# A new order of row gathers, two blocks fewer visited early, and other places for the steps woven between them

## The reference

```python
s_top, i_top = lax.top_k(scores, PEER_TOPK)          # twice 128 keys, 16 of each
best, pos = lax.top_k(cand, PEER_TOPK)               # 16 of the 256 pairs
u = u_tab[ib]
act = gelu(einsum("td,thkd->thk", tb, u))            # a dot product for each row
out = einsum("thk,thkd->td", gb * act, v_tab[ib])
x = x + out
```

```python
u = h @ w_up                                         # 1024 -> 5632, 22 pairs of 128 columns
u = up[:, :-2]*conv_w[0] + up[:, 1:-1]*conv_w[1] + up[:, 2:]*conv_w[2] + conv_b
return (silu(a) * v) @ w_down                        # 2816 -> 1024
```

## Time and profile before

| what | us |
|---|---|
| median of 3 runs | 1692.13 (1692.06 to 1692.37) |
| profiled execution | 1692.13 |
| its span | 1690.2 |
| TensorE matmuls busy | 1488.3 (88%) |
| VectorE busy | 1043.8 (62%) |
| GpSimd busy | 745.1 (44%) |
| ScalarE busy | 529.0 (31%) |
| mean granted TensorE clock | 0.942 |

### The profile page before, as it was taken

One profiled execution on the slowest core, in us unless ns is written; L12 is line 12 of the kernel. 1 busy time (PEld: TensorE's weight loads), 2 busy tenths in 40 slices (PEclk: granted clock), 3 DMA queues, 4 the chain that ended last, 5 costly groups with the idle time before them and its releaser, 6 DMA issues.

```text
span 1690.2 us, 22536 instructions
## 1 busy us (share of the span) xinstructions
PE 1488.3 (88%) x8510; PEld 1046.8 (62%) x8510; DVE 1043.8 (62%) x2210; ACT 529.0 (31%) x839; POOL 745.1 (44%) x676
## 2 busy tenths in 40 slices
PE   8999999846566777885999999998699999999999
PEld 7997675734222333432855555544399986799987
DVE  5865633797597866787677775431244157568864
ACT  6653331211121121113322210002133164466652
POOL 0025220476667777775346665655000013027650
PEclk9999999978787789997999999999799999999999
DMA  7447860698999999999999999999668756635551
GB/s 277 150 150 314 316 230 25 249 394 295 401 406 371 378 381 390 405 406 355 335 386 383 378 374 401 340 342 337 230 211 285 265 215 257 216 134 191 172 195 42
DMA packets 161308, 489.51 MB, mean 290 GB/s; under 512 B 10160, under 2 KB 14000, under 8 KB 158000
## 3 DMA queue, kind: packets, MB, share of 16 engines
q0 software_dynamic: 73728, 268.47, 41.4%
q1 hardware_dynamic: 87472, 219.60, 35.7%
HBM read 486.98 MB, written 1.05 MB: 289 GB/s over the span
## 4 chain that ended last, share of the span: by engine, by line
PE 60%; POOL 10%; DMA 9%; DVE 8%; issue 5%; ACT 2%; another core or an unknown queue 1%; DVEq 0%; ACTq 0%; POOLq 0%
PE ps L761 59%; POOL arena L3096 8%; DMA arena<-in_peer_v,cl 5%; DVE arena L2028 2%; POOL wring L3096 2%; PE ps L765 2%; DMA wring<-in_ups 1%; DMA wring<-in_peer_v,cl 1%; DVE arena L1642 1%; DVE arena L1648 1%; ACT arena L2439 1%; DMA arena<-in_peer_u,arena 1%; DMA wring<-in_attn_w_qkv 0%; DVE arena L1645 0%
## 5 line engine op out<-in xcount | busy, mean ns | idle before, releaser
L761 PE MATMUL ps<-arena,wring 128*32 128x512 f32 (+6 forms) x3048 | 713.0, 461 | 101.7 <-DMA arena<-in_peer_v,cl 85.8
L761 PEld LDWEIGHTS ps<-arena,wring 128*128 128x128 f32 (+1 forms) x3048 | 402.7, 172 | 390.8 <-DMA arena<-in_peer_v,cl 154.0
L3096 POOL DMA_INDIRECT arena<-in_peer_u,arena x214 | 243.2, 1136 | 257.2 <-PE ps L761 117.4
L2028 DVE CUSTOM_DVE_ANT_0 arena<-arena 128x1024 f32<-128x1024 f32 x214 | 255.9, 1225 | 118.8 <-DMA arena<-in_peer_u,arena 101.1
L3096 POOL DMA_INDIRECT arena<-in_peer_v,cl x214 | 229.8, 1074 | 96.7 <-issue 62.0
L2439 ACT ACT_TABLE_LOAD x68 | 87.2, 1283 | 354.6 <-DVE arena L2028 162.7
L1648 DVE SCALAR_TENSOR_TENSOR cvs<-ps,vec,cvs 128x255 f32<-128x255 f32 (+3 forms) x240 | 105.3, 439 | 59.5 <-ACT cvs L2439 47.3
L761 PE MATMUL ps<-hhl,wh 128*128 128x256 f32 (+1 forms) x528 | 126.2, 322 | 0.6 <-POOL hhl L3106 0.4
L761 PEld LDWEIGHTS ps<-arena 128*128 128x128 f32 (+1 forms) x708 | 88.4, 198 | 50.5 <-issue 29.5
L761 PE MATMUL ps<-arena 128*128 128x128 f32 (+4 forms) x708 | 100.1, 295 | 22.1 <-ACT arena L2442 8.0
L1642 DVE TENSOR_TENSOR wl<-wring,wh 128x2048 fp32r<-128x2048 f32 (+1 forms) x42 | 92.1, 2193 | 37.7 <-ACT wh L2442 36.8
(11 more groups left out here) (279 smaller groups left out, 2219.4 us busy)
## 6 DMA issues: line engine op xcount, KB each, us to landing
wring<-in_ups SPq DMA_DIRECT2D x38, 2048.0 KB
wring<-in_ada SPq DMA_DIRECT2D x24, 2048.0 KB, 11.8
wring<-in_ffn_w_down SPq DMA_DIRECT2D x12, 2048.0 KB
wring<-in_w_in SPq DMA_DIRECT2D x8, 2048.0 KB
wring<-in_ffn_w_down SPq DMA_DIRECT2D x6, 1536.0 KB
wring<-in_peer_wq SPq DMA_DIRECT2D x4, 2048.0 KB
wring<-in_attn_w_qkv SPq DMA_DIRECT2D x4, 2048.0 KB
wring<-in_w_out SPq DMA_DIRECT2D x2, 2048.0 KB
```

Source lines behind the costliest of these rows:

```text
L761: return pe.matmul(o, l, r, start=start, stop=stop)
L2028: ve.tensor_tensor_reduce(out=o, in0=o, in1=h2[:, t, :], scale=1.0, scalar=0.0, op0=MUL, op1=ADD, accum_out=dots[j % 2][:, k:k + 1]).then_ ...
L3096: po.indirect_dma_start(out=ring[n % NR], out_offset=None, in_=table, in_offset=bass.IndirectOffsetOnAxis(ap=which, axis=0)).then_inc(S[f" ...
```

## The change

It has four parts. `EARLY_BLOCKS` goes from 10 to 8, so two blocks have one visit "both" instead of two visits, and one load of weights falls away. The gathers get a new order: up to row 215 as before; then five times 8 "v" and 4 "u", with which the "v" rows of half 0 end at row 271 instead of 291; then 28 more "u" without a "v" (with the four before them 32 "u" in a row, rows 272 to 303); then 4 and 4 in turn; and 48 "v" at the end. The places of the steps move: "ctx" visits 13 rests apart, the short steps from rest 292 and 1.9 rests apart, "a" visits 2.3, "both" visits 6.4, down projection 3.3 and 2.4, the last steps 1 rest apart. With these the first "a" visit is at rest 318, as before. And `woven()` takes at most one step at a rest, and none at a rest where the second half of a visit is due.

```diff
--- before.py
+++ after.py
@@ -100,7 +100,7 @@
     MUL, ADD, SUB, MAX, MIN, BYP = ALU.mult, ALU.add, ALU.subtract, ALU.max, ALU.min, ALU.bypass
     ctx = ExitStack()
 
-    EARLY_BLOCKS, BESIDE = 10, ()
+    EARLY_BLOCKS, BESIDE = 8, ()
 
     GOES_ON = {
         "p_gp": ("p_hT", 4), "p_h2T": ("p_gp", 1), "p_xc": ("p_h2T", 4), "p_zb": ("p_xc", 4), "p_xT": ("p_zb", 1), "p_zbb": ("p_xT", 2), "p_xTb": ("p_zbb", 1), "p_cum": ("p_g", 1), "p_crow": ("p_cum", 1),
@@ -368,8 +368,11 @@
 
         u = [("u", n // 128, n % 128) for n in range(256)]
         v = [("v", s, n) for s in range(8) for n in range(32)]
-        both = [x for g in range(0, 256 - AHEAD, 4) for x in v[g:g + 4] + u[AHEAD + g:AHEAD + g + 4]]
-        return u[0:AHEAD] + both + v[256 - AHEAD:]
+        first = [x for g in range(0, 128 - AHEAD, 4) for x in v[g:g + 4] + u[AHEAD + g:AHEAD + g + 4]]
+        g0 = 128 - AHEAD
+        first += [x for g in range(5) for x in v[g0 + 8 * g:g0 + 8 * g + 8] + u[128 + 4 * g:132 + 4 * g]]
+        then = [x for g in range(20) for x in v[128 + 4 * g:132 + 4 * g] + u[176 + 4 * g:180 + 4 * g]]
+        return u[0:AHEAD] + first + u[148:176] + then + v[208:]
 
     ROWS = fetched()
     NTH = {x: n for n, x in enumerate(ROWS)}
@@ -483,11 +486,11 @@
         places = [5 * (k + 1) // 2 for k in range(11)] + [44 + 56 * (k - 10) // 10 for k in range(11, 34)]
         n = 178
         for f in range(BEFORE_A + 2):
-            places.append(int(n))
-            n += 12.5 if f < BEFORE_A else 0.5
-        n = max(n, 311)
-        for lengths in ([0.5] * 14, [2.1] * EARLY_BLOCKS, [6.6] * (22 - EARLY_BLOCKS), [1] * 2,
-                        ([3.0] * 8 + [2.3] * 4) * 2, [2] * 11):
+            places.append(n)
+            n += 13 if f < BEFORE_A else 2
+        n = max(n, 292)
+        for lengths in ([1.9] * 14, [2.3] * EARLY_BLOCKS, [6.4] * (22 - EARLY_BLOCKS), [1] * 2,
+                        ([3.3] * 8 + [2.4] * 4) * 2, [1] * 11):
             for length in lengths:
                 places.append(int(n))
                 n += length
@@ -512,7 +515,7 @@
                 if n == half:
                     next(context, None)
                     half = None
-                while half is None and steps < len(places) and n >= places[steps]:
+                elif steps < len(places) and n >= places[steps]:
                     steps += 1
                     if next(context, None) == "half":
                         half = n + 3
```

## The result

The changed kernel took **1704.43 us** (median of 3, 1704.10 to 1706.31) against 1692.13: 1.0069 times the kernel before, 95% interval 1.0053 to 1.0087. Forecast were 1702 us and "slower". The profiled execution was the quickest of the changed kernel, 1694.82 us with a span of 1693.0, so it is read for lengths of stretches, not for the total.

A forecast was written before the change was run, and what follows sets the result against it. Limits in turn: DMA engines to 751 us, nothing full to 811.2, TensorE to 1131.3, then a mixed tail. 1692.1 + 7 (burst) + 15.4 (TensorE) - 12.4 (tail) = 1702 us, 0.6% slower; range 1697 to 1709.

The forecast's parts named there:

- an "a" visit before 800 us: Sign of being wrong: "a" visits starting before 800 us would mean VectorE kept up; forecast start 818 us.
- a gap in TensorE behind the "a" visits: Sign of being wrong: TensorE gaps after the "a" visits, from a late load or late VectorE taps.
- Part 1: Up to the sum of token half 0: the sum comes at 753 instead of 784 us, 31 us early.
- Just covered: Rows 216 to 275: TensorE's load goes from 85% to 98%, at 0.32 us a record; 1.5 us taken for this.
- I give no gain for them: Before the sum: two fewer early context visits and one 2.1 MB load, under full DMA engines, gain nothing.
- Part 2: Sum to first "a" visit: VectorE's 62 us plus 3 us waits make 65; first "a" visit 7 us later.
- the rival of a faster burst: Sum to first "a" visit: row supply sets the pace, 42 us; decides under 52 us; total 1679; chance 0.15.
- every gather waits out a dot product: Rival, sum to first "a" visit: 28 gathers take 69 us, 4 us more than 65; total 1706; chance 0.05.
- Part 3: First "a" visit to end of down projection: TensorE is the limit, 335.4 us, 15.4 us longer.
- the short steps stall the full VectorE: Rival: hand-over waits and a lower TensorE clock at the "a" visits, some 10 us more, 1712; chance 0.12.
- Part 4: Tail after the down projection: fewer rows left, 8 gathers instead of 12, 56.7 us, 12.4 us shorter.
- cost 21 us where TensorE is the limit: From the first "a" visit on: cost of two blocks visited once, against visits saved mostly under the DMA engines.

The follow-up runs named there:

- e1: The changed kernel again, unaltered: 1706.90 us, 1.0100 times the kernel before.
- e12: The changed kernel once more, unaltered, in the third set: 1694.92 us, 1.0098 times the kernel before.
- e9: The kernel before with 8 instead of 10 early blocks, nothing else, in the third set: 1673.81 us, 0.9976.
- e10: The kernel before with 8 early blocks and the change's later spacing, old row order: 1684.66 us, 1.0030.
- e4: The changed kernel with dot products of rows 272 to 303 over 512 of 1024 columns, leaving out half of those sums: 1691.76 us, 1.0015.
- e3: The kernel before with the new order and early short steps, ten blocks, old later spacing, context visits 11.2 rests apart: 1698.57 us, 1.0052.
- e6: The changed kernel with the later spacing of the kernel before: 1689.65 us, 1.0080.
- e11: The changed kernel with the old later spacing, again, in the third set: 1687.51 us, 1.0050.
- e7: The kernel before with 6 early blocks, nothing else: 1679.49 us, 1.0009.

## Why the prediction was right, and where its steps were wrong

The total and the sign held: +9.9 us forecast, +12.3 measured with the pair of medians at the head, +17.9 and +16.9 in e1 and e12, beside medians of their own sets, which is the far end of the forecast's own range (1709 us is +17). Two of its terms did not hold, and they lie on opposite sides. Two of its signs of being wrong came, too: an "a" visit before 800 us (799.4 in the changed kernel's trace, though 808.4 and 802.2 in e1 and e12), and a gap in TensorE behind the "a" visits, by VectorE's taps. Its first sentence misreads: TensorE is at 4 to 8 tenths from 338 to 804 us, not near nine; the sum doesn't rest on that.

**Part 1, the sum 31 us early: right.** It is 95.8 to 99.4 us behind row 216 instead of 128.4, where 97.5 were forecast, and the DMA share stayed at 1.03. "Just covered", at 98% of TensorE, was too dear: it had 75.6 us of work in 98.8, and a record of the "v" rows cost 45.6/174 = 0.26 us there, not 0.32. What was wrong is "I give no gain for them" about the two visits and the load that fall away. In the old order this stretch is set by bytes: 128.4, 122.5 and 118.6 us with ten, eight and six blocks, at a share of 1.03 each time, in which the queues moved 52.0, 49.8 and 48.5 MB. At 0.405 MB a us the 2.2 and 1.3 MB less are 5.4 and 3.3 us of the 5.9 and 3.9. In the changed kernel no such gain is left over against the forecast: TensorE also waits 3.7 us for the weights and 7.8 for the top-k in these rows.

**Part 2, VectorE sets the burst: right; 65 us: mis-sized, 54 measured.** The dot products and the gathers behind the sum in the changed kernel, columns as in the earlier trace rows:

```profile
...
L2031 DVE CUSTOM_DVE_ANT_0 arena<-arena x21: 1214/1222/1245, 744.5 to 798.8; 128x1024 f32<-128x1024 f32 x21
L2031 DVE CUSTOM_DVE_ANT_0 wring<-wring,arena x4: 1221/1225/1231, 746.9 to 778.3; 128x1024 f32<-128x1024 f32 x4
...
```

```profile
...
L3099 POOL DMA_INDIRECT arena<-in_peer_u,arena x19: 934/957/1988, 745.7 to 798.4; - x19
...
```

From the sum to the first "a" visit there are 24 to 25 dot products, not 28: 25 x 1.15 = 29 us, where I had 32 to 34. The larger error is in the rest. I took the 43.9 us of the earlier trace rows less 13 dot products, 29 us, as what the short steps and their surroundings cost. But that window starts 32 us ahead of the old sum, with taps and top-k parts that do not follow it. From the sum on, the old order has 18.0 us of VectorE work in 27.1 (e9's first row), 3 of them for the two or three dot products there, so 15 for the short steps. 15 + 29 + 8 for parts of the top-k (one whole one, not two sixths of one) are 52 us, and 51.7 were measured; waits were 2.1 us, not 3. At 54 us the stretch is nearer to the 52 at which the prediction let the rival of a faster burst decide than to its own 65, and what VectorE had to do decided all the same. So the first "a" visit is not 7 us late but 2 to 6 us early: 149.9 to 153.5 us behind row 216, for 155.7.

The rival that the burst runs at the pace of the rows (42 us) is wrong: it took halved dot products to come to 44.6. So is the one that every gather waits out a dot product: the middle duration of these 19 "u" gathers is 957 ns, the least 934, where VectorE is 96% busy (1086 ns for the four that go to the other ring places). The rule of the Trainium skill that I had weighed (SBUF — State Buffer, section Who interferes with whom) does not show in the middle value; single gathers of up to 1988 ns occur.

**Part 3, TensorE's counted work: right to 1 us in the old order; in the new one +15.4 was 10 to 14 us short.** Forecast were 335.4 us. With the change's blocks and spacing in the old order (e10) the part takes 34.4 + 166.5 + 135.2 = 336.1, a little by luck: it has one group of "v" fewer than was counted (23 for 24, 1.9 us) and 3 us of idle time. In the new order it takes 344.7 to 348.1 (changed, e1, e12), against 319.2 before. Of the changed kernel's 344.7 us, 6.7 are idle time, for which the prediction had none; the clock is most of the rest. What I did not see is the lower clock behind the burst, and waits for VectorE in the new order with the lower clock again behind them. First the clock. TensorE, idle for 7.6 us directly ahead of the first "a" visit and mostly idle for 46 us before that, starts it at a granted clock of 0.50, the lower level of 1.2 GHz, and has 1.00 from 803.6 us on. Its first records, and the window (columns as in the earlier trace rows):

```profile
...
799.42 0.99 PE L764 MATMUL ps<-arena,wring 128*128 128x120 f32 x3 [7.59 <-ACT arena L2442]
```

```profile
...
799.40:803.60 4.20, 4.18 (x19) 4.18 (x20) 4.03 (x13) 0.00 (x0) 1.25 (x2) 0.50 0.90 323
...
```

The eight "a" visits take 35.6 to 38.7 us behind the burst, at 0.92 to 0.94, and 34.4 in e10 at 0.95: 1 to 4 us. I had this in the rival "the short steps stall the full VectorE", beside larger waits that did not come. Then VectorE. It has 134.0 us of work in the "both" part for 126.9 in e10, and at the end of that part the chain from TensorE over ScalarE's bias to VectorE's taps lies bare. TensorE, then VectorE, in the changed kernel around the start of the down projection:

```profile
...
1003.48 0.27 PE L768 MATMUL ps<-cbase,wt 128*128 128x128 f32 x1
1008.10 1.28 PE L764 MATMUL ps<-arena,wring 128*128 128x376 f32 x2 [4.36 <-DVE cbase L1651]
```

```profile
...
1002.37 0.55 DVE L1645 TENSOR_TENSOR arena<-cvs 128x376 f32<-128x376 f32 x1
1005.19 2.55 DVE L1651 SCALAR_TENSOR_TENSOR cbase<-ps,vec,cbase 128x376 f32<-128x376 f32 x4 [2.27 <-ACT cbase L2442]
...
```

TensorE waits 4.36 us, until the taps end at 1007.7; before, it had no idle time there. With 1.1 us for a late gather and 0.5 for the top-k, that makes the "both" part 4 to 7 us longer than in e10, as many "v" groups in both. This isn't VectorE's work carried over from the burst. In e4, with the burst's dot products halved and the first "a" visit 8 to 12 us earlier behind row 216, TensorE waits the same 4.36 us at the same place, and the part still takes 343.1 us:

```profile
...
1000.75 2.81 PE L764 MATMUL ps<-arena,wring 128*128 128x376 f32 x4 [4.36 <-DVE cbase L1651]
```

And e3 has the whole burst, but the later places of before, and its "both" part is no longer than before (145.1 us for 145.5). In e6 and e11, the new order with eight blocks and the old later spacing, the wait is another one (5.5 us for the top-k in e11). So these waits come with how the new order and the places of the steps fall together in the written order of the engines; which row or step makes them was not taken apart. The down projection is 1 to 2 us longer than in e10. It has one group of "v" more than in e10 (1.9 us) and not e10's 2.4 us of idle time, and its 336 records take 111.8 us instead of 109.9. That is the clock behind the wait of 4.4 us: TensorE starts the down projection at 0.54 for 3.7 us, and at 0.50 for 6.2 and 5.9 us in e1 and e12, where the 336 records take 113.2 and 113.0. In e10 it is 1.00 throughout.

```profile
...
L764 PE MATMUL ps<-arena,wring 128*128 128x376 f32 x336 | 111.8, 488 | 4.4 <-DVE cbase L1651 4.4
...
```

```profile
...
1008.10:1011.80 3.70, 3.70 (x7) 2.04 (x8) 3.42 (x9) 0.25 (x1) 1.55 (x2) 0.54 1.01 363
...
```

**Part 4, -12.4 us: right** (-10.6 to -13.0), and by its own reason, fewer rows left at the end of the down projection: 492 gathers have gone out by then instead of 476. The drain is 21.9 to 23.2 us where 24 were forecast. The chain ahead of it is 35.2 to 36.4 us and not 32.7, since the wait of 6.9 us and the slow records behind it use up what the two groups fewer give. I failed to apply the reason, fewer rows left, to the parts. It holds for anything that makes the stages ahead longer: with eight blocks alone 488 have gone out and the tail is 15.0 to 15.7 us shorter. The drain is paced by gathers that go out and land, as the chain that ended last shows for e9:

```profile
...
1156.28 0.93 POOL arena L3096
...
1159.99 5.96 DMA arena<-in_peer_v,cl
...
1167.36 10.06 DMA arena<-in_peer_v,cl
...
```

So my sentence in part 3, that two blocks visited once "cost 21 us where TensorE is the limit", is true of the stage and false of the kernel. Less the two "a" visits, 7.7 us, 13.3 were forecast, and the trace has +8.7 from the first "a" visit to the end of the "both" part (199.8 us for 191.1). The load and the visits give 5.9 back ahead of the sum and the tail more than the rest. With six blocks the drain is down to 3.6 us and the gain ends (e7).

**In short.** Forecast: +7 (burst) + 15.4 (TensorE) - 12.4 (tail). By the changed kernel's trace: -3.1 + 25.5 - 10.6 = +11.8. The first term was 10 us too high and the second 10 us too low. That the errors cancel is chance: the first is a wrong base for VectorE's work in the burst (54 us for 65), the second the idle time and the lower clock in the new order, for which the prediction had nothing.

**What stays open.** Which of the new order's places makes TensorE wait for VectorE at the start of the down projection was not taken apart. Why the table's totals against the kernel before lie up to 9 us under the medians was not found. The gain of eight blocks is 8.3 us in one set and 4.2 in another, on different chips; why was not found. The new order with the short steps left where they were was not tried, nor ten blocks under the new order with a spacing that keeps the weights in time.

**The best version** is the kernel before with eight early blocks and nothing else: 0.9942 and 0.9976 times its time, in two sets, and 21.1 us under the changed kernel in the last.

## What to carry to other kernels

Cut the window of before at the event that the change moves; a window that starts earlier carries work that does not follow. When rows are moved under a fixed script, look also behind the moved ones, at each place where another engine waits for what the script now puts late, and price the lower clock behind each such wait. A tail in which a queue drains is slack for everything ahead of it: price a longer stage by what the tail gives back, and look how much drain is left, since there the gain stops.

## What the runs showed of the hardware that was not expected

The same kernel before has medians of 1692.13, 1688.96, 1678.73 and 1678.01 us in the four sets, up to 0.8% apart, more than most effects here; only ratios within a set can be used. In the traces this scatter sits ahead of row 216, where the gathers run under full DMA engines: 333 to 346 us from the first gather on, for the same order of rows. The stretches behind it repeat within 3.6 us. And a TensorE that had 15.8 us of work in 53.8 (granted clock 0.63) does its next eight visits at 0.94, where 14 us in 27 (0.75) are followed by 1.00 (e9) or, with the later spacing alone, by 0.95 (e10), so the idle share ahead is not all of it. In these runs a single wait was enough: behind 4.4 us of idle time at the end of a fully busy part the granted clock was 0.54 for 3.7 us (0.50 for some 6 us in e1 and e12), behind 6.9 us in the tail 0.50 for 5.8 us.
